# Differential attention scores as 64-row matmuls on two row groups, two slots' worth at a time in every second slot

## What is computed

```python
def block(args):                      # 128 query positions at a time
    ...
    s = jnp.einsum('ibhqd,ibhkd->ibhqk', qblk, k).astype(jnp.float32) * scale + bias   # i: the two maps
    s = jnp.where(rel >= 0, s, -jnp.inf)
    p = jax.nn.softmax(s, axis=-1)
    a = p[0] - lam * p[1]
    return jnp.einsum('bhqk,bhkd->bhqd', a.astype(v.dtype), v)
```

## Time and profile before

| what | us |
|---|---|
| median of 3 runs | 2472.44 |
| lowest and highest run | 2469.86, 2473.18 |
| the profiled execution | 2473.61 |
| its span (first to last instruction) | 2472.0 |
| TensorE matmuls busy | 2286.7 (93%) |
| VectorE busy | 1348.7 (55%) |
| ScalarE busy | 1208.2 (49%) |
| GpSimd busy | 766.3 (31%) |

### The profile page before, as it was taken

One profiled execution on the slowest core, in us unless ns is written; L12 is line 12 of the kernel. 1 busy time (PEld: TensorE's weight loads), 2 busy tenths in 40 slices (PEclk: granted clock), 3 DMA queues, 4 the chain that ended last, 5 costly groups with the idle time before them and its releaser, 6 DMA issues. The chain is left out here.

```text
span 2472.0 us, 36835 instructions
## 1 busy us (share of the span) xinstructions
PE 2286.7 (93%) x11480; PEld 1838.0 (74%) x11480; DVE 1348.7 (55%) x2806; ACT 1208.2 (49%) x1639; POOL 766.3 (31%) x686
## 2 busy tenths in 40 slices
PE   6999999997999999999979995799999999999980
PEld 5788889996677777767658885577888888788760
DVE  6321121104777776767445776676655566766663
ACT  5111111113777777777644443565554555656553
POOL 0000000003887878777600112222222222222220
PEclk9999999998999999999989997899999999999995
DMA  5433334224643454344036444599887788988957
GB/s 197 162 112 135 110 127 128 62 66 109 147 120 90 101 135 101 83 100 132 18 136 204 136 128 162 206 354 349 280 263 255 264 254 272 322 285 276 330 146 289
DMA packets 207632, 441.51 MB, mean 179 GB/s; under 512 B 19081, under 2 KB 56113, under 8 KB 205490
## 3 DMA queue, kind: packets, MB, share of 16 engines
q1 hardware_dynamic: 188530, 379.46, 46.8%
q0 software_dynamic: 19008, 60.91, 9.9%
HBM read 338.55 MB, written 101.76 MB: 178 GB/s over the span
## 5 line engine op out<-in xcount | busy, mean ns | idle before, releaser
L1495 DVE TENSOR_TENSOR gu_lo<-gu_raw,gu_hi 128x2048 fp32r<-128x2048 f32 x128 | 293.2, 2291 | 124.5 <-issue 87.1
L682 DVE TENSOR_SCALAR_CACHE_REDUCE p_ring<-ps_s 128x512 f32<-128x512 f32 (+6 forms) x352 | 277.5, 793 | 117.5 <-PE ps_s L753 106.4
L622 POOL TENSOR_TENSOR p_ring<-p_ring 128x512 f32<-128x512 f32 (+2 forms) x192 | 334.5, 1742 | 16.0
L647 ACT ACTIVATE p_ring<-p_ring,shift 128x1152 f32<-128x1152 f32 (+15 forms) x256 | 305.7, 1197 | 17.1 <-DVE shift L698 17.1
L790 PE MATMUL ps_o<-aT,v_st 128*128 128x512 f32 (+3 forms) x640 | 285.5, 530 | 0.0
L636 ACT ACTIVATE aT<-ps_t 128x512 f32<-128x512 f32 (+1 forms) x320 | 169.1, 531 | 166.0 <-PE ps_t L775 164.9
L1572 PE MATMUL ps_g<-gu_hi,xT_lo 128*128 128x512 f32 x720 | 236.0, 409 | 7.5 <-DVE xT_lo L1510 7.5
L1435 ACT ACTIVATE gu_hi<-gu_raw 128x2048 fp32r (+1 forms) x128 | 237.8, 1913 | 10.0 <-PE ps_g L1572 5.4
L1572 PE MATMUL ps_g<-gu_lo,xT_hi 128*128 128x512 f32 x720 | 227.4, 397 | 0.0
L1572 PE MATMUL ps_g<-gu_hi,xT_hi 128*128 128x512 f32 x720 | 227.0, 396 | 0.0
L619 POOL TENSOR_SCALAR p_ring<-p_ring,coef 128x512 f32<-128x512 f32 (+2 forms) x192 | 168.2, 876 | 123.6 <-DVE coef L711 123.2
(11 more groups left out here) (217 smaller groups left out, 4324.4 us busy)
## 6 DMA issues: line engine op xcount, KB each, us to landing
gu_raw<-in_moe_w_gate SPq DMA_DIRECT2D x128, 512.0 KB
gu_raw<-in_moe_w_up SPq DMA_DIRECT2D x128, 512.0 KB
d_raw<-in_moe_w_down SPq DMA_DIRECT2D x64, 1024.0 KB
qk<-stage SPq DMA_DIRECT2D x64, 512.0 KB, 2.8
q_first<-qk SPq DMA_DIRECT2D x64, 256.0 KB, 5.1
q_second<-qk SPq DMA_DIRECT2D x64, 256.0 KB, 5.2
w_raw<-in_diff_w_in POOLq DMA_DIRECT2D x12, 1024.0 KB, 6.6
k<-qk SPq DMA_DIRECT2D x8, 1024.0 KB, 12.7
```

The source lines that it names most:

```text
L622: pool.tensor_tensor(p0(r, c0, c1), p0(r, c0, c1), p1(r, c0, c1), ALU.add).then_inc(mixed, 1)
L647: nc.scalar.activation(p, p, ACT.Exp, bias=shift[:, r % 8, m:m + 1], accum_out=sums[:, r % 8, m:m + 1]).then_inc(raised, 1)
L682: ins = nc.vector.tensor_scalar(p(r, k0, k0 + far), ps_s[:, c % 2, 0:far], SCALE, None, ALU.mult, ALU.max, accum_out=top[:, r % 4, m, col: ...
L1495: nc.vector.tensor_tensor(gu_lo[:, j * GC:(j + 1) * GC], raw(half, j), gu_hi[:, j * GC:(j + 1) * GC].bitcast(F32), ALU.subtract).then_inc( ...
```

## The change

- **Layout.** q and k now keep the layout of device memory: map 0 in partitions 0 to 63, map 1 in 64 to 127, the high and the low part beside each other. A quad's q comes in one transfer of half the bytes, a head's k in one transfer in place of two.
- **Matmuls.** For each 512 keys three products are made (q_lo k_hi, q_hi k_lo, q_hi k_hi; q_lo k_lo is left out), each as two matmuls of 64 rows, map 0's on partitions 0 to 63 and map 1's on 64 to 127. The two write different halves of `ps_s`, which is now [128, 2, 2, 512].
- **Pieces.** A piece is at most 512 keys, the odd remainder of a row first, and the two maps alternate: 640 pieces in 320 pairs. `score(c)` makes a pair, which needs `taken` to have reached the pair before the last.
- **Slots.** Pieces are handed out in even slots only, with a lead raised by 4, so that an even slot has about two pairs and an odd slot none.
- **VectorE** takes each piece of 512; the maxima need five columns of `top` in place of three.

The hunks on the first load of k and q in `project`, on waits of DMA counts in `take`, and on the places in SBUF are left out here.

```diff
@@ -35,11 +35,8 @@
 
 def load_q_quad(eng, scratch, place, h, j, landed):
 
-    for hl in range(2):
-        for lanes in (slice(0, HALF), slice(HALF, P)):
-            eng.dma_start(place[lanes, hl].bitcast(F32),
-                          scratch["qk"][h, hl, :, j * 512:(j + 1) * 512].rearrange("(m d) t -> d m t", m=2)
-                          ).then_inc(landed, 16)
+    eng.dma_start(place.bitcast(F32), scratch["qk"][h, :, :, j * 512:(j + 1) * 512].rearrange("l p t -> p l t")
+                  ).then_inc(landed, 16)
 
 
 def project(nc, io, keep, scratch, sem):
...
@@ -395,6 +390,7 @@
     SCALE = HALF ** -0.5
     NEAR = 2 * P
     WIDE = 1024
+    PIECE = 512
     QUADS = (FIRST_QUAD, 0, 3, 1)
     LEAD0, LEAD = 72, 104
     P0, P1 = 86 * 256, 24 * 256
@@ -405,10 +401,12 @@
     pieces = []
     for r, (g, i) in enumerate(rows):
         w = (i + 1) * P
-        for m in range(2):
-            head = WIDE // 2 if w <= 3 * WIDE // 2 else WIDE
-            for k0, n in [(0, w)] if w <= WIDE else [(0, head), (head, w - head)]:
+        k0 = 0
+        while k0 < w:
+            n = (w - k0 - 1) % PIECE + 1
+            for m in range(2):
                 pieces.append((r, m, k0, n))
+            k0 += n
     units = [(g, k) for g, (h, j) in enumerate(quads) for k in range(4 * j + 4)]
     NG, NR, NC, NU = len(quads), len(rows), len(pieces), len(units)
     first_piece = [min(c for c in range(NC) if pieces[c][0] == r) for r in range(NR)]
@@ -431,9 +429,10 @@
     slots, c, scored_cost, turned_cost = {}, 0, 0.0, 4 * BEGIN
     for n in range(BEGIN, END):
         start = c
-        while c < NC and scored_cost < turned_cost + min(LEAD, LEAD0 + max(0, n)):
-            scored_cost += pieces[c][3] / (2 * P)
-            c += 1
+        ahead = turned_cost + min(LEAD, LEAD0 + max(0, n)) + 4
+        while n % 2 == 0 and c < NC and scored_cost < ahead:
+            scored_cost += pieces[c][3] / P
+            c += 2
         slots[n] = range(start, c)
         turned_cost += tiles(n) if 0 <= n < NU else 4
     slot_of = {c: n for n, cs in slots.items() for c in cs}
@@ -488,12 +487,13 @@
         p1_ring = keep["p1_ring"]
         aT = sb("aT", [P, A_RING, 512])
         oT = sb("oT", [P, 512])
-        sb("q_first_place", [P, 2, 2, 512], F32R)
-        q_st = (keep["q_first"], sb("q_second", [P, 2, 2, 512], F32R))
+        sb("q_first_place", [P, 2, 512], F32R)
+        q_st = (keep["q_first"], sb("q_second", [P, 2, 512], F32R))
+        sb("w_rest_place", [P, 2, D])
         sb("near_place", [P, 2, NEAR])
         near = keep["near_both"]
         o_sb = sb("o_sb", [P, 2, 4, P])
-        top = sb("top", [P, 4, 2, 3])
+        top = sb("top", [P, 4, 2, 5])
         shift = sb("shift", [P, 8, 2])
         sums = sb("sums", [P, 8, 2])
         inv = sb("inv", [P, 32, 2])
@@ -503,7 +503,7 @@
         nil = sb("nil", [P, D // 4])
         edots = sb("edots", [P, 2])
         neg_lam = sb("neg_lam", [P, 1])
-        ps_s = ctx.enter_context(nc.psum_tensor("ps_s", [P, 2, WIDE], F32))
+        ps_s = ctx.enter_context(nc.psum_tensor("ps_s", [P, 2, 2, PIECE], F32))
         ps_t = ctx.enter_context(nc.psum_tensor("ps_t", [P, 2, 512], F32))
         ps_o = ctx.enter_context(nc.psum_tensor("ps_o", [P, 2, 512], F32))
         ident = keep["ident"]
@@ -531,9 +531,8 @@
 
         def load_k(eng, h):
 
-            for hl in range(2):
-                eng.dma_start(k_st[h % 2][hl * HALF:(hl + 1) * HALF].bitcast(F32),
-                              scratch["qk"][HEADS + h, hl].rearrange("(m d) t -> d m t", m=2)).then_inc(k_in[h % 2], 16)
+            eng.dma_start(k_st[h % 2][:, :, :].bitcast(F32), scratch["qk"][HEADS + h].rearrange("l p t -> p l t")
+                          ).then_inc(k_in[h % 2], 16)
 
         def load_near(eng, h):
 
...
@@ -678,24 +677,24 @@
                 p = (p0, p1)[m]
                 dve.wait_ge(scored, c + 1)
                 if far:
-                    col = 0 if not last else 1
-                    ins = nc.vector.tensor_scalar(p(r, k0, k0 + far), ps_s[:, c % 2, 0:far], SCALE, None,
+                    col = 3 - ((i + 1) * P - k0 - n) // PIECE
+                    ins = nc.vector.tensor_scalar(p(r, k0, k0 + far), ps_s[:, c // 2 % 2, m, 0:far], SCALE, None,
                                                   ALU.mult, ALU.max, accum_out=top[:, r % 4, m, col:col + 1])
                 if n_near:
                     ins = nc.vector.tensor_tensor_reduce(
-                        p(r, k0 + far, k0 + n), ps_s[:, c % 2, far:n], near[:, h % 2, NEAR - n_near:NEAR],
-                        SCALE, LOWEST, ALU.add, ALU.max, top[:, r % 4, m, 2:3])
+                        p(r, k0 + far, k0 + n), ps_s[:, c // 2 % 2, m, far:n], near[:, h % 2, NEAR - n_near:NEAR],
+                        SCALE, LOWEST, ALU.add, ALU.max, top[:, r % 4, m, 4:5])
                 ins.then_inc(taken, 1)
 
             def peaks(r):
 
                 i = rows[r][1]
-                first = 0 if i >= 8 else 1 if i >= 2 else 2
+                first = 4 - ((i + 1) * P + PIECE - 1) // PIECE if i >= 2 else 4
                 if r >= 8:
 
                     dve.wait_ge(raised, 2 * (r - 8) + 2)
                 dve.wait_ge(taken, last_piece[r] + 1)
-                nc.vector.tensor_reduce(shift[:, r % 8, :], top[:, r % 4, :, first:3], AX.X, ALU.max,
+                nc.vector.tensor_reduce(shift[:, r % 8, :], top[:, r % 4, :, first:5], AX.X, ALU.max,
                                         negate=True).then_inc(peaked, 1)
 
             def weigh(r):
@@ -735,24 +734,26 @@
         @block.tensor
         def _(pe):
             def score(c):
-                r, m, k0, n = pieces[c]
+
+                r, _, k0, n = pieces[c]
                 g, i = rows[r]
                 h = quads[g][0]
                 if c == first_piece[r]:
                     if r % 16 == 0:
-                        pe.wait_ge(k_in[h % 2], 48 * (h // 2 + 1))
+                        pe.wait_ge(k_in[h % 2], 32 * (h // 2 + 1))
                     if r % 4 == 0:
-                        pe.wait_ge(q_in[g % 2], 64 * (g // 2 + 1))
-                if c >= 2:
-
-                    pe.wait_ge(taken, c - 1)
+                        pe.wait_ge(q_in[g % 2], 16 * (g // 2 + 1))
+                if c >= 4:
+
+                    pe.wait_ge(taken, c - 2)
                 a = i % 4
-                for j in range(0, n, 512):
-                    e = min(512, n - j)
-                    for hl in (1, 0):
-                        mm = pe.matmul(ps_s[:, c % 2, j:j + e], q_st[g % 2][:, hl, m, a * P:(a + 1) * P],
-                                       k_st[h % 2][:, m, k0 + j:k0 + j + e], start=hl == 1, stop=hl == 0)
-                mm.then_inc(scored, 1)
+                for k, (ql, kl) in enumerate(((1, 0), (0, 1), (0, 0))):
+                    for m in range(2):
+                        lanes = slice(m * HALF, (m + 1) * HALF)
+                        mm = pe.matmul(ps_s[:, c // 2 % 2, m, 0:n], q_st[g % 2][lanes, ql, a * P:(a + 1) * P],
+                                       k_st[h % 2][lanes, kl, k0:k0 + n], start=k == 0, stop=k == 2)
+                        if k == 2:
+                            mm.then_inc(scored, 1)
 
             def ps_t_free(t):
 
@@ -799,7 +800,7 @@
                 mm.then_inc(turned, 1)
 
             for n in range(BEGIN, END):
-                for c in slots[n]:
+                for c in slots[n][::2]:
                     score(c)
                 if 0 <= n < NU:
                     turn(n)
```

More of the change, by code:

```diff
@@ L144, in _ @@
             sp.wait_ge(moved, 32)
-            for hl in range(2):
-                sp.dma_start(k0[hl * HALF:(hl + 1) * HALF].bitcast(F32),
-                             scratch["qk"][HEADS, hl].rearrange("(m d) t -> d m t", m=2)).then_inc(k0_in, 16)
+            sp.dma_start(k0[:, :, :].bitcast(F32), scratch["qk"][HEADS].rearrange("l p t -> p l t")).then_inc(k0_in, 16)
             def store_v(b, first):
@@ L159, in _ @@
             sp.wait_ge(filled, QK_FILLS + (VB - 1) * TILES + 1)
-            load_q_quad(sp, scratch, keep["q_first"], 0, FIRST_QUAD, sem("b_q_in0"))
+            load_q_quad(sp, scratch, keep["q_first"][:, :, :], 0, FIRST_QUAD, sem("b_q_in0"))
             sp.dma_start(keep["near_both"][:, 0, :], scratch["near"][0]).then_inc(k0_in, 16)
@@ L548, in load_q @@
             h, j = quads[g]
-            load_q_quad(eng, scratch, q_st[g % 2], h, j, q_in[g % 2])
+            load_q_quad(eng, scratch, q_st[g % 2][:, :, :], h, j, q_in[g % 2])
         @block.sync
@@ L670, in take @@
                     if r % 16 == 0:
-                        dve.wait_ge(k_in[h % 2], 48 * (h // 2 + 1))
+                        dve.wait_ge(k_in[h % 2], 32 * (h // 2 + 1))
                     if p0_frees[r] >= 0:
@@ L1707, in build @@
         with nc.sbuf_tensor("hn_place", [P, 2, KC, SEQ], F32):
-            with nc.sbuf_tensor("q_first", [P, 2, 2, 512], F32R) as q_first:
+            with nc.sbuf_tensor("q_first", [P, 2, 512], F32R) as q_first:
```

(2 more changed lines are left out.)

## The result

| what | before | after |
|---|---|---|
| median, us | 2472.7 (4 runs) | 2496.7 (4 runs, 2495.7 to 2498.6) |
| ratio to before, 95% interval | | 1.0103 [1.0090, 1.0116] |
| profiled execution, its span | 2473.6, 2472.0 | 2498.6, 2496.9 |
| last matmul of the attention starts at | 1247.8 | 1268.5 |

The forecast was 2443 us and faster; the kernel became 1% slower. Of the two profiles' 25 us, 21 lie in the attention.

A forecast was written before the change was run, and what follows sets the result against it. TensorE was taken as the bound in the attention's middle. Products -38, waits +10 and the start -1 summed to -29 us: 2444.6 from the profiled 2473.6, 2443 as median, range 2420 to 2520.

The forecast's parts named there:

- What bounds the kernel: Middle of the attention: TensorE is the bound, busy 581 of 590 us, so a microsecond off it is one off the kernel.
- Side by side: Score products: the two 64-row matmuls of a product run at the same time, a 512 product costing 0.237 us.
- The rival's 2590 us: Score matmuls: pairs don't run side by side, 118 us lost, about 2590 us without a drain; chance 0.13.
- The products, term of -38 us: Score products behind the start: 241 us before, 203 us after, a gain of 38 us.
- the best case of 61: Score products: weight loads side by side and narrow products at 0.177, 0.123 and 0.11 give 180 us, a gain of 61.
- Changes of array shape, term of 0: Ends of score blocks: 288 changes between 128-row and 64-row work cost 0 each, with 0.26 us as end of the range.
- The rival "drains at every change": TensorE at each change of shape: drain and uncovered load, up to 75 us, 2489 to 2518 us; chance 0.33, whole or part.
- Waits for VectorE, +10: Score blocks on TensorE: third pairs wait for VectorE, 32 us in place of about 22, so 10 more; bounds 0 and 20.
- VectorE's own work hidden: VectorE in the attention: 21 to 40 us more work, hidden in 171 us to spare, except in the start.
- the start: Start of the attention, where VectorE sets the pace: net -1 us, bounds -5 and +4.
- the loads of q: SyncE's transfers for q, one in place of four and half the bytes: no effect, since the middle waits only 0.6 us.
- Signs that were named: In the trace: 0.24 us between paired records, block ends over 0.10 us meaning slower, waits about 30 us, middle 561 us.

The follow-up runs named there:

- the run of shapes: A separate kernel of matmuls alone, 128-row and 64-row in runs and in turn; two matmuls and two pairs took 1.33 us where a stream would take 0.91.
- the cap: The changed kernel with at most two pairs in a block behind the start: 2461.3 us, ratio 0.9962 to the kernel before.

## Why the prediction was wrong, by its own steps

- **What bounds the kernel:** right. TensorE stayed the bound, and its 21 us in the attention are the kernel's.
- **Side by side:** right, and the largest assumption of the sum. A pair of 64-row matmuls costs what one matmul of 128 rows costs. (The rival's 2590 us left out the +10 and -1 of the other terms; with them it is 2599.)
- **The products, term of -38 us:** mis-sized. They gained 59. The narrow products were priced at two loads in a row (0.21 us); the loads of a pair go together (0.11 us at 128 columns), which was the best case of 61. The estimate by the Trainium skill's 3.07x (TensorE: Matmul & The Clock Gate, "Measured speedup vs the span model"), 1.5 of 2, doesn't hold here: 24 pairs of 512 columns took 5.75 us, 24 matmuls of 128 rows 5.60.
- **Changes of array shape, term of 0: this is the step that failed.** "I take 0, by the rows that lie nearest in the program" took the changes between kinds of matmul for neighbours of a change of shape. They aren't: a change of kind is free, a change of shape costs 0.21 us in the run of shapes, and in the kernel a block's two cost 0.36 us, 52 us over 144 blocks. The bound from the other side, 0.26 for a tail and a load, was nearly it; the tail counts 0.10, not 0.16, and the load 0.11. The break-even was put at 0.10 per change, and the measured price is about twice that. The rule of the Trainium skill (TensorEngine Tiling (Array Packing), "Key Properties"), that changing the mode drains and changing the tile doesn't, is what the run of shapes shows on both sides: 0.21 us for the one, nothing for the other.
- **The rival "drains at every change", 2489 to 2518 us:** right in mechanism and side. At the measured price it would have given, with the other terms as predicted, 2443 + 52 = 2495. That this is so near to 2497 is partly luck: the products gained 21 us more, and the waits and the clock took 18 more.
- **Waits for VectorE, +10:** mis-sized, +25. The step that two pairs never wait held, in 68 of 69 blocks. The third pair was put at 1.1 us for 512-128-512 and costs 1.8 (mean over 13 blocks, 3.78 less 0.30 and 1.70). Twelve of them wait 1.5 to 1.6 us, because their first pair is a row's last, which takes VectorE 1.5 us and not 1.2, and it begins up to 0.16 us late. The other waits 4.2 us: there VectorE came 2.0 us late from `weigh`, and the clock fell. Three more blocks before 671 us were held up by `weigh`, by 0.4 to 1.7 us; none behind that. The cause, third pairs, is shown by the cap: it took 36 us away, more than the 25 added, since it leaves 10 us of waits where the kernel before had 19, and no half clock.
- **VectorE's own work hidden, the start, the loads of q:** right in mechanism. VectorE is busy 468 us in the attention where it was 450, so 18 us more and not 21 to 40; the start didn't change, where -1 was put; no wait for q is left.
- **Signs that were named:** 0.23 us between products, and over 0.10 us at the ends of a block, are what the trace shows. Waits of about 30 us in some 40 places became 44 us in 41 blocks. The middle, from the first transpose to the end of the last score block, took 611 us in place of 561.

## What to carry to other kernels

Before using row groups inside a stream of full-array work, count the entries and exits, not the matmuls: here a round trip cost 0.36 to 0.42 us, and the two pairs of 512 columns in a block save 0.46, so that block just about pays for itself. A block should hold no more results than the consumer's buffers have free; one condition that kept the third pair out was worth more (36 us) than all of the row groups (about 4 us in that schedule). An operation's nearest neighbour in a program isn't its nearest in kind: the trace had no row for it, and already a price at the middle of the two bounds, 0.13 us x 288 = 37 us against the 29 gained, would have given the right side.

## What the runs showed of the hardware that was not expected

- 64-row matmuls on different row groups run together even when issued three and three, or two and two: 47 in 5.84 us, 0.12 us each, against 0.23 for those of one group alone (22 in 5.15 us).
- The weight loads of a pair run together as well: 0.11 to 0.12 us a pair at 128 columns, as for one matmul (0.11).
- TensorE's clock fell in the longest wait. In the kernel after TensorE waited 3.25 us for VectorE until 656, and the granted clock was 0.54 from 654.4 to 661.3, the lower level (1.2 GHz) for nearly all of it; before the change the same stretch ran at 1.00. The stretch after the change, in the columns of the earlier trace rows:

```profile
654.40:661.30 6.90, 5.24 (x13) 2.67 (x14) 3.85 (x20) 3.96 (x9) 6.73 (x5) 0.54 0.75 271
```

In it one `add_v` took 1.91 us in place of 1.02. The table's 3 us are an estimate from this: the work of some 6 us took twice its time.
